# Differential attention in an encoder trunk: the turned map's low part ahead of the combination, the last map's reciprocal between the two stacks, and the copy of K's low part on ScalarE

## The chip, the cores and the metric

The kernel runs as one launch on one core of a Trainium2 chip. The metric is the device time of that launch in microseconds (us), median of several runs. The engines are TensorE (PE, with PEld for its weight loads), VectorE (DVE), ScalarE (ACT), GpSimd (POOL) and SyncE (SP, which starts the DMAs). Each engine works through its own list of instructions in order and waits at semaphores.

## The reference

Two layers over 1024 positions of width 1024, all in float32. Layer 0 mixes tokens by differential attention (8 heads, two softmax maps a head), layer 1 by neighbourhood attention; a gated feed-forward part with a convolution follows each. The change touches only the differential attention:

```
q = q.reshape(B, S, H, 2, dh) * (dh ** -0.5)      # H = 8 heads, 2 maps, dh = 64
s = einsum('bqhcd,bkhcd->bhcqk', q, k)            # two score maps, c = 0, 1
s = s - slopes[h] * |q_pos - k_pos|               # penalty by distance
p = softmax(s, axis=-1)
a = p[:, :, 0] - lam * p[:, :, 1]                 # the combination of the two maps
o = einsum('bhqk,bkhe->bqhe', a, v)               # v has 2*dh = 128 columns
o = rms_norm(o, subln_g) * (1.0 - lambda_init)
```

## The kernel before, in words

TensorE multiplies in a format that rounds its operands, so each operand is held in two parts, a high part (the rounded value) and a low part (the rest), and a product is the sum of two or three matmuls. ScalarE makes the high part by a copy, VectorE the low part by a subtraction.

The attention stage takes one head after another, and a head in 8 steps, step t for the 128 queries of tile t. The order on every engine is written out by hand in a function `head` for each; heads 1 to 6 run it in a loop, head 0 and head 7 have copies of their own. In step t of head h:

- PE: `score(t)` makes the two score maps (4 matmuls of 512 columns for map 0, then 4 for map 1), each after the exponential of its map of the step before is done, since there is one PSUM buffer for each map. Then come 12 or 24 matmuls of the next head's projections (`CHUNKS`), in odd steps the product with V of a pair of tiles (`weigh`), and at the step's end the transposition of the combined map of step t-1 (`turn_map(t-1)`, into the one PSUM buffer `da_tb`). Step 2 also turns V (`turn_v`) between its scores and its projections, through the same buffer. `turn_v` needs the low part of map 0 out of the buffer, and `turn_map(1)` needs V's.
- DVE: `combine` (L616: map 0 divided by its sum plus the scaled map 1, both in SBUF), `take_low` (L608: low part of the transposed map t-2, from PSUM and SBUF), in odd steps `finish_o` (L624), then `bias` twice (L660: adds the penalty and finds the row minimum, maps 0 and 1), in even steps L628, in step 2 the low part of V (L608), last the reciprocal of the row sums (L674), which waits for both exponentials.
- ACT: when due, a projection's result out of PSUM (`take`, L490) and two readings of the product with V (L505, L506), then `take_high` (L495: high part of the transposed map t-2), then the exponentials of both maps (L547). In step 2 V's high part (L495) lies between the two.
- POOL: `scale_map` (L278) multiplies map 1 by its reciprocal and minus lambda, after the reciprocal; `combine` waits for it. In steps 0, 3 and 6 a weight tile for a later head is split right behind it: its high part (L270, here called wh) and its low part (L272, here called wl).

At the end of step 7 the next head's operands are stacked. ACT copies the high parts of K and Q for each map c (L515, L516), POOL doubles K's (L296) and halves the penalty strip (L314), and DVE (`stacks`, L630 to L641) makes for each c K's low part (L635), Q's low part (L638) and a copy of K's low part in the other 64 partitions (L641). Then comes the reciprocal of step 7. `score(0)` of the next head waits for all of that; 10 projection matmuls (`EARLY`) stand ahead of it in heads 0 to 6, none in head 7. In head 7 `combine` already comes after the two biases.

Of the kernel before, what the change touches and what calls it, by code (L numbers as in the profile page):

```python
# [15 lines left out]
F32 = mybir.dt.float32  # L16
F32R = mybir.dt.float32r
ALU = mybir.AluOpType
ACT = mybir.ActivationFunctionType
# [56 lines left out]
def diff_attention_stage(nc, x, w_qkv, lam_vec, subln_g, rpb, Z, OT, XTh, XTl, ident, S, lambda_init, shared_raw, next_tiles):  # L76
# [12 lines left out]
    DH = 64  # L89
    H = D // P  # L90
    QT = S // P
# [14 lines left out]
    with ExitStack() as ctx:  # L106
# [5 lines left out]
        raw = m.sb("raw", [P, 3, S])  # L112
        QS = m.sb("QS", [P, 2, S], F32R)
# [357 lines left out]
        @block.scalar  # L471
        def _(act):
            nc.scalar.preload_act_table(ACT.Exp)
            act.wait_ge(iota_done, 1)

            nc.scalar.activation(strip[:], strip[:], ACT.Abs, scale=0.5).then_inc(strip_ready, 1)

            def x_high_part(t):
                act.wait_ge(x_turned, t + 1)
                nc.scalar.activation(XTh[:, :, t * P:(t + 1) * P], xp[t], ACT.Copy).then_inc(x_high, 1)  # L480

            def w_high_part(j):

                act.wait_ge(w_in[j % 2], 16 * (j // 2 + 1))
                nc.scalar.activation(wh[:, j], wraw[:, j % 2], ACT.Copy).then_inc(w_high, 1)

            def take(h, j):

                act.wait_ge(proj_done, ORDER.index(j) + 1 if isinstance(h, int) and h == 0 else 6 * h + j + 1)
                nc.scalar.activation(raw[:, j // 2, (j % 2) * BANK:(j % 2 + 1) * BANK], bank(h, j)[:], ACT.Copy,  # L490
                                     scale=-(DH ** -0.5) if j < 2 else 1.0).then_inc(proj_out, 1)

            def take_high(i, out):
                act.wait_ge(turned, i + 1)
                nc.scalar.activation(out, tb[:], ACT.Copy).then_inc(t_high, 1)  # L495

            def take_map(h, qt):
                q = qt // 2
                if not (isinstance(h, int) and h == 0 and q < 2):
                    act.wait_ge(pv_done, 4 * h + q - 1)  # L500
                take_high(t_index(h, qt), ATh[:, q % 2, :, (qt % 2) * P:(qt % 2 + 1) * P])

            def ready_o(i):
                act.wait_ge(pv_done, i + 1)
                nc.scalar.activation(sq[:], pb[:, 0:QW], ACT.Square).then_inc(sq_ready, 1)  # L505
                nc.scalar.activation(og[:], pb[:, 0:QW], ACT.Copy, scale=gsub[:, 1:2]).then_inc(og_ready, 1)  # L506

            def stacks(h, after):

                act.wait_ge(proj_out, 6 * h + 4)  # L510
                if after:
                    act.wait_ge(scored[1], 8 * h)
                for c in range(2):
                    a = slice(c * DH, (c + 1) * DH)
                    nc.scalar.activation(KH[a, c], raw[a, 1], ACT.Copy).then_inc(stack_high, 1)  # L515
                    nc.scalar.activation(QS[a, c], raw[a, 0], ACT.Copy).then_inc(stack_high, 1)  # L516

            def head(h, first, last):
                for t in range(QT):
                    n = 8 * h + t  # L520
                    if t in TAKE and t and not last:
                        if TAKE[t] == 0:
                            act.wait_ge(stack_low, 4 * h + 4)
                        if TAKE[t] == 4:
                            act.wait_ge(turned, 9 * h + 2)
                        take(h + 1, TAKE[t])
                    if t == 0 and not first:
                        take(h, TAKE[0])
                    if t % 2 == 0 and (t > 2 or not first):
                        ready_o(4 * h + t // 2 - 2)  # L530
                    if t >= 2:
                        take_map(h, t - 2)
                    elif not first:
                        take_map(h - 1, t + QT - 2)
                    if t == QT - 1 and not last:
                        stacks(h + 1, True)
                    for c in range(2):
                        if t == 2 and c == 1:
                            if not first:
                                act.wait_ge(pv_done, 4 * h)  # L540
                            take_high(9 * h + 1, Vh[:])
                        act.wait_ge(biased[c], n + 1)
                        if t >= 2:
                            act.wait_ge(turned, t_index(h, t - 2) + 1)
                        elif not first:
                            act.wait_ge(turned, t_index(h - 1, t + QT - 2) + 1)
                        nc.scalar.activation(E[:, t % 2, c], Sc[c][:], ACT.Exp, scale=-1.0, bias=mn[:, t % 2, c:c + 1],  # L547
                                             accum_out=den[:, t % 2, c:c + 1]).then_inc(exped[c], 1)

            for t in range(QT // 2):  # L550
                x_high_part(t)
            w_high_part(0)
            w_high_part(1)
            take(0, 0)
            for t in range(QT // 2, 3 * QT // 4):
                x_high_part(t)
            w_high_part(2)
            take(0, 2)
            for t in range(3 * QT // 4, QT):
                x_high_part(t)  # L560
            for j in ORDER[2:4]:
                take(0, j)
            stacks(0, False)
            for j in ORDER[4:]:
                take(0, j)
            act.wait_ge(lam_dots, 2)
            nc.scalar.activation(lams[:, 2:4], lams[:, 0:2], ACT.Exp).then_inc(lam_exps, 1)
            act.wait_ge(g_ready, 1)
            head(0, True, False)
            with act.Fori(1, H - 1) as h:  # L570
                head(h, False, False)
            head(H - 1, False, True)
            ready_o(4 * H - 2)
            take_map(H - 1, QT - 2)
            take_map(H - 1, QT - 1)
            ready_o(4 * H - 1)

        @block.vector
        def _(dve):
# [30 lines left out]
            def take_map(h, qt):  # L610
                at = (slice(None), (qt // 2) % 2, slice(None), slice((qt % 2) * P, (qt % 2 + 1) * P))
                take_low(t_index(h, qt), ATh[at], ATl[at])

            def combine(n, b):
                dve.wait_ge(scaled, n + 1)
                nc.vector.scalar_tensor_tensor(out=E[:, b, 0], in0=E[:, b, 0], scalar=rden[:, b, 0:1], in1=E[:, b, 1],  # L616
                                               op0=ALU.mult, op1=ALU.add).then_inc(combined, 1)
# [9 lines left out]
                dve.wait_ge(sum_done, i + 1)  # L627
                nc.vector.tensor_scalar(ms[:], pb[:, QW:QW + 2], 1.0 / P, RMS_EPS, ALU.mult, ALU.add).then_inc(ms_ready, 1)  # L628

            def stacks(h):  # L630

                for c in range(2):
                    a, b = slice(c * DH, (c + 1) * DH), slice((1 - c) * DH, (2 - c) * DH)
                    dve.wait_ge(stack_high, 4 * h + 2 * c + 1)
                    nc.vector.tensor_tensor(out=KL[a, c], in0=raw[a, 1], in1=KH[a, c].bitcast(F32),  # L635
                                            op=ALU.subtract).then_inc(stack_low, 1)
                    dve.wait_ge(stack_high, 4 * h + 2 * c + 2)
                    nc.vector.tensor_tensor(out=QS[b, c], in0=raw[a, 0], in1=QS[a, c].bitcast(F32),  # L638
                                            op=ALU.subtract).then_inc(stack_low, 1)
                    dve.wait_ge(stack_low, 4 * h + 2 * c + 1)  # L640
                    nc.vector.tensor_copy(KL[b, c], KL[a, c].bitcast(F32)).then_inc(kl_dup, 1)  # L641

            def head(h, first, last):
                for t in range(QT):
                    n = 8 * h + t
                    if (t or not first) and not last:
                        combine(n - 1, (t - 1) % 2)
                    if t >= 2:
                        take_map(h, t - 2)
                    elif not first:  # L650
                        take_map(h - 1, t + QT - 2)
                    if t >= 5 and t % 2 == 1:
                        finish_o(h, (t - 5) // 2)
                    elif t % 2 == 1 and not first:
                        finish_o(h - 1, (t + 3) // 2)
# [12 lines left out]
                    if t == 2:  # L668
                        take_low(9 * h + 1, Vh[:], Vl[:])
                    if t == QT - 1 and not last:  # L670
                        stacks(h + 1)
                    dve.wait_ge(exped[0], n + 1)
                    dve.wait_ge(exped[1], n + 1)
                    nc.vector.reciprocal(rden[:, t % 2], den[:, t % 2]).then_inc(inverted, 1)  # L674

            stacks(0)
            dve.wait_ge(lam_exps, 1)

            nc.vector.scalar_tensor_tensor(out=neglam[:], in0=lams[:, 3:4], scalar=-lambda_init, in1=lams[:, 2:3],
# [1257 lines left out]
```

## Time and profile before

| | us |
|---|---|
| median of 3 runs | 2939.55 |
| their range | 2937.84 to 2942.13 |
| the profiled execution: its time | 2941.45 |
| its span, first to last instruction | 2939.6 |
| PE busy / DVE / ACT / POOL | 2761.2 / 1646.7 / 993.7 / 1244.3 |

The attention stage takes about the first 680 us; its heads 1 to 6 lie between 136 and 593 us and take about 76 us each. PE's busy time counts overlapping, pipelined matmuls, so it says that PE is seldom without work, not that it is at its peak. What matters for the change is where PE waits inside a head, and for which instruction of which engine.

### The profile page before, as it was taken

The page shows a single profiled execution, that of the slowest core. Times are in us where ns is not written, and L with a number is a line of the kernel's source. Part 1 is how long each engine was busy: PE and PEld are TensorE (multiplying, and loading weights), DVE is VectorE, ACT ScalarE, POOL GpSimd, SP SyncE. Part 2 cuts the span into 40 slices and gives each one's busy share as a digit, 9 for nine tenths or more (in the row PEclk, how much of TensorE's full clock was granted, in tenths as well). Part 3 has the DMA queues.
Part 4 walks back from the last instruction along what each step waited for, and adds up shares of the span by engine and source line. Part 5 has one row for each costly group of instructions (what it writes and reads, how often), then busy time and mean ns, then how long its engine had stood idle before and what let it go on. Part 6 is the DMA issues. An engine that isn't in the chain of part 4 may idle for free. (4 is left out here: it accounts for less than half of the span.)

```text
span 2939.6 us, 36441 instructions
## 1 busy us (share of the span) xinstructions
PE 2761.2 (94%) x13387; PEld 2300.0 (78%) x13387; DVE 1646.7 (56%) x2106; ACT 993.7 (34%) x1402; POOL 1244.3 (42%) x890
## 2 busy tenths in 40 slices
PE   7999999967899999999988999998789999999998
PEld 6788888856788888888877888887668888888886
DVE  3666666663564444444473777777475444444447
ACT  3544555442231122222233555555323111222222
POOL 2444444333563333333354566555357233333335
PEclk9999999988999999999999999999899999999999
DMA  3000001225111111111121221211602111111111
GB/s 117 26 27 24 29 29 35 56 67 190 41 47 43 51 54 46 50 48 45 50 79 42 64 51 44 48 44 22 213 13 75 43 43 52 55 43 50 50 43 72
DMA packets 212649, 163.16 MB, mean 56 GB/s; under 512 B 34939, under 2 KB 194251, under 8 KB 212555
## 3 DMA queue, kind: packets, MB, share of 16 engines
q1 hardware_dynamic: 212411, 161.38, 18.6%
q8 instruction: 59, 0.97, 0.1%
q10 hardware_dynamic: 144, 0.52, 0.1%
q14 instruction: 35, 0.29, 0.0%
HBM read 137.24 MB, written 24.64 MB: 55 GB/s over the span
## 5 line engine op out<-in xcount | busy, mean ns | idle before, releaser
L1131 PE MATMUL ff_ph<-XTh,WH 128*128 128x512 f32 x1408 | 549.7, 390 | 6.9 <-PEq L41 6.9
L1131 PE MATMUL ff_ph<-XTl,WH 128*128 128x512 f32 x1408 | 548.9, 390 | 0.0
L1131 PE MATMUL ff_ph<-XTh,WL 128*128 128x512 f32 x1408 | 548.7, 390 | 0.0
L1289 DVE SCALAR_TENSOR_TENSOR ff_C<-ff_H,ff_par,ff_C 128x1024 f32<-128x1024 f32 x88 | 206.5, 2346 | 548.1 <-ACT ff_C L1233 548.1
L1069 POOL TENSOR_SCALAR WH<-raw_weights 128x1024 fp32r<-128x1024 f32 x128 | 142.3, 1111 | 845.6 <-PE ff_ph L1131 488.9
L1071 POOL TENSOR_TENSOR WL<-raw_weights,WH 128x1024 fp32r<-128x1024 f32 x128 | 328.9, 2570 | 10.7
L1131 PEld LDWEIGHTS ff_ph<-XTh,WH 128*128 128x128 f32 x1408 | 265.0, 188 | 62.7 <-issue 7.6
L1131 PEld LDWEIGHTS ff_ph<-XTh,WL 128*128 128x128 f32 x1408 | 265.0, 188 | 55.5
L1131 PEld LDWEIGHTS ff_ph<-XTl,WH 128*128 128x128 f32 x1408 | 265.1, 188 | 54.9
L1229 ACT ACTIVATE ff_H<-ff_ph,ff_par 128x1024 f32<-128x1024 f32 x88 | 98.4, 1118 | 553.6 <-PE ff_ph L1131 553.6
L1282 DVE TENSOR_TENSOR X<-ff_po,X 128x512 f32<-128x512 f32 x288 | 191.6, 684 | 102.5 <-PE ff_po L1145 102.5
L1145 PE MATMUL ff_po<-WH 128*128 128x512 f32 x576 | 228.3, 396 | 4.7 <-DVE X L1282 0.2
L1145 PE MATMUL ff_po<-WH,WL 128*128 128x512 f32 x576 | 224.4, 390 | 0.0
L1145 PE MATMUL ff_po<-WL,WH 128*128 128x512 f32 x576 | 224.4, 390 | 0.0
L547 ACT ACTIVATE da_E<-da_S,da_mn 128x1024 f32<-128x1024 f32 x128 | 142.9, 1117 | 226.4 <-DVE da_mn L660 223.7
L1526 POOL TENSOR_SCALAR na_E<-na_E,na_rden 128x512 f32<-128x512 f32 x128 | 103.8, 811 | 204.8 <-DVE na_rden L1868 204.7
L1612 PE MATMUL na_pa<-XTh,na_wh 128*128 128x512 f32 x360 | 146.1, 406 | 18.8 <-ACT na_raw L1731 11.8
L278 POOL TENSOR_SCALAR da_E<-da_E,da_rden,da_neglam 128x1024 f32<-128x1024 f32 x64 | 76.6, 1197 | 199.6 <-DVE da_rden L674 199.6
L347 PE MATMUL da_pa<-XTh,da_wh 128*128 128x512 f32 x360 | 151.7, 421 | 10.0 <-POOL da_wl L272 3.8
L660 DVE CUSTOM_DVE_ANT_0 da_S<-da_S,da_strip 128x1024 f32<-128x1024 f32 x128 | 153.8, 1241 | 9.2 <-PE da_S L361 8.2
L1243 ACT ACTIVATE WH<-ff_C 128x1024 fp32r<-128x1024 f32 x44 | 46.8, 1063 | 306.5 <-PE ff_po L1145 268.9
L1612 PE MATMUL na_pa<-XTl,na_wh 128*128 128x512 f32 x360 | 143.9, 400 | 0.0
(224 smaller groups left out, 5990.7 us busy)
## 6 DMA issues: line engine op xcount, KB each, us to landing
raw_weights<-in_ffn_w_in SPq DMA_DIRECT2D x88, 512.0 KB, 3.8
raw_weights<-in_ffn_w_out SPq DMA_DIRECT2D x44, 512.0 KB, 3.5
raw_weights<-in_attn_w_qkv SPq DMA_DIRECT2D x24, 512.0 KB
raw_weights<-in_na_w_qkv SPq DMA_DIRECT2D x24, 512.0 KB, 4.2
wo_oraw<-heads_t SPq DMA_DIRECT2D x16, 512.0 KB, 4.6
rpb_rows<-da_rows SPq DMA_DIRECT2D x2, 3840.0 KB, 26.4
na_B<-rpb_rows SPq DMA_DIRECT2D x32, 224.0 KB, 4.2
da_E<-in_x SPq DMA_DIRECT2D x8, 512.0 KB, 6.5
```

The lines of the kernel that those rows point to most:

```text
L347: last = nc.tensor.matmul(out[:], w[:, j // 2, k], x[:, k, t0:t0 + BANK], start=(i == 0), stop=(i == 3 * KT - 1))
L547: nc.scalar.activation(E[:, t % 2, c], Sc[c][:], ACT.Exp, scale=-1.0, bias=mn[:, t % 2, c:c + 1], accum_out=den[:, t % 2, c:c + 1]).then_i ...
L660: nc.vector.tensor_tensor_reduce(out=Sc[c][:], in0=Sc[c][:], in1=strip[:, (QT - 1 - t) * P:(QT - 1 - t) * P + S], scale=1.0, scalar=3.0e38 ...
L1069: nc.gpsimd.tensor_scalar(wh[:, slot], wraw[:, raw_slot], 1.0, 1.0, ALU.mult, ALU.mult).then_inc(w_high, 1)
L1071: nc.gpsimd.tensor_tensor(out=wl[:, slot], in0=wraw[:, raw_slot], in1=wh[:, slot].bitcast(F32), op=ALU.subtract).then_inc(w_low, 1)
L1131: last = nc.tensor.matmul(out[:, at], wt[:, slot, k * P:(k + 1) * P], x[:, k, at], start=(k == 0 and n == 0), stop=(k == KT - 1 and n == 2))
L1145: last = nc.tensor.matmul(po[r % 4][:], a[:, f, t * P:(t + 1) * P], wt[:, slots[f], half * BANK:(half + 1) * BANK], start=(f == 0 and n == ...
L1229: nc.scalar.activation(H[:, parity, 1:S + 1], ph[parity][:].rearrange("p k n -> p (k n)"), ACT.Identity, bias=par[:, 0, bass.ds(idx, 1)])
L1282: nc.vector.tensor_tensor(out=at, in0=po[r % 4][:], in1=at, op=ALU.add).then_inc(added, 1)
L1289: nc.vector.scalar_tensor_tensor(out=c, in0=h[:, 0:S], scalar=tap[1], in1=c, op0=ALU.mult, op1=ALU.add).then_inc(conv_link, 1)
L1526: nc.gpsimd.tensor_scalar(E[:, b], E[:, b], rden[:, b:b + 1], 1.0, ALU.mult, ALU.mult).then_inc(scaled, 1)
L1612: last = nc.tensor.matmul(out[:], w[:, j // 2, k], x[:, k, t0:t0 + BANK], start=(i == 0), stop=(i == 3 * KT - 1))
```

## The change

Three edits in the attention stage. On DVE `take_low` of map t-2 now stands ahead of `combine` of map t-1. The stacks of the last step are cut in two, with the reciprocal between them: stack 0, reciprocal, stack 1. The copy of K's low part (L641) goes from DVE to ACT: for c = 0 behind the two exponentials of step 7, for c = 1 in step 0 of the next head, behind `take_high`. The waits on semaphores keep their meaning.

```diff
+            def double_low(h, c):
+                a, b = slice(c * DH, (c + 1) * DH), slice((1 - c) * DH, (2 - c) * DH)
+                act.wait_ge(stack_low, 4 * h + 2 * c + 1)
+                nc.scalar.activation(KL[b, c], KL[a, c].bitcast(F32), ACT.Copy).then_inc(kl_dup, 1)
...
                         take_map(h - 1, t + QT - 2)
                     if t == QT - 1 and not last:
                         stacks(h + 1, True)
+                    if t == 0 and not first:
+                        double_low(h, 1)
...
+                    if t == QT - 1 and not last:
+                        double_low(h + 1, 0)
...
             stacks(0, False)
+            for c in range(2):
+                double_low(0, c)
...
-            def stacks(h):
-
-                for c in range(2):
...
-                    dve.wait_ge(stack_low, 4 * h + 2 * c + 1)
-                    nc.vector.tensor_copy(KL[b, c], KL[a, c].bitcast(F32)).then_inc(kl_dup, 1)
+            def stacks(h, c):
...
                     n = 8 * h + t
-                    if (t or not first) and not last:
-                        combine(n - 1, (t - 1) % 2)
                     if t >= 2:
                         take_map(h, t - 2)
                     elif not first:
                         take_map(h - 1, t + QT - 2)
+                    if (t or not first) and not last:
+                        combine(n - 1, (t - 1) % 2)
...
                     if t == QT - 1 and not last:
-                        stacks(h + 1)
+                        stacks(h + 1, 0)
                     dve.wait_ge(exped[0], n + 1)
                     dve.wait_ge(exped[1], n + 1)
                     nc.vector.reciprocal(rden[:, t % 2], den[:, t % 2]).then_inc(inverted, 1)
+                    if t == QT - 1 and not last:
+                        stacks(h + 1, 1)
```

On DVE, steps 5 and 6 of a head in the loop. Before (`da_E` is the combination, `da_ATl` the low part, `da_S` the bias):

```order
L674 RECIPROCAL da_rden<-da_den 128x2
L616 SCALAR_TENSOR_TENSOR da_E<-da_E,da_rden 128x1024
L607 REGISTER_ALU
L608 TENSOR_TENSOR da_ATl<-da_tb,da_ATh 128x8x128
L27 REGISTER_ALU
L660 ISA da_S,da_mn<-da_S,da_strip 128x1024
```

and after, where each line number is 7 to 11 higher:

```order
L681 RECIPROCAL da_rden<-da_den 128x2
L618 REGISTER_ALU
L619 TENSOR_TENSOR da_ATl<-da_tb,da_ATh 128x8x128
L627 SCALAR_TENSOR_TENSOR da_E<-da_E,da_rden 128x1024
L27 REGISTER_ALU
L667 ISA da_S,da_mn<-da_S,da_strip 128x1024
```

The low part and the combination have changed places between the reciprocal and the bias, in every step of heads 0 to 6. On DVE at the end of step 7, before:

```order
L635 TENSOR_TENSOR da_KL<-da_raw,da_KH 64x1024
L637 REGISTER_ALU
L638 TENSOR_TENSOR da_QS<-da_raw,da_QS 64x1024
L641 CAST da_KL<-da_KL 64x1024
L634 REGISTER_ALU
L635 TENSOR_TENSOR da_KL<-da_raw,da_KH 64x1024
L637 REGISTER_ALU
L638 TENSOR_TENSOR da_QS<-da_raw,da_QS 64x1024
L641 CAST da_KL<-da_KL 64x1024
L674 RECIPROCAL da_rden<-da_den 128x2
```

and after:

```order
L644 TENSOR_TENSOR da_KL<-da_raw,da_KH 64x1024
L646 REGISTER_ALU
L647 TENSOR_TENSOR da_QS<-da_raw,da_QS 64x1024
L681 RECIPROCAL da_rden<-da_den 128x2
L643 REGISTER_ALU
L644 TENSOR_TENSOR da_KL<-da_raw,da_KH 64x1024
L646 REGISTER_ALU
L647 TENSOR_TENSOR da_QS<-da_raw,da_QS 64x1024
L692 REGISTER_ALU
L692 COMPARE_AND_BRANCH
```

The reciprocal has moved ahead of the second stack and the two copies are gone; the second stack now runs straight into the loop's branch.

## Rows read from the trace of the kernel before

**Rows 1.** Windows of two heads; columns: stretch, length, PE busy, clock, DMA

```profile
364.70:440.60 75.90, 72.20 (x400) 1.00 0.09 28
440.60:517.20 76.60, 73.60 (x401) 0.98 0.16 40
```

**Rows 2.** Waits of PE, 130 to 570 us; columns: total us, times, longest

```profile
PE da_tb L376 <- DVE da_ATl L608: 9.4, 6, 1.6
PE da_S L360 <- ACT da_E L547: 5.0, 6, 0.9
PE da_tb L369 <- DVE da_Vl L608: 3.1, 4, 0.8
PE da_S L360 <- DVE da_KL L641: 2.3, 6, 0.4
```

**Rows 3.** Timeline, PE, heads 4 and 5; columns: start, us, instruction, [idle before]

```profile
390.52 0.48 PE L360 MATMUL da_S<-da_KH,da_QS 128*128 128x512 f32 x1
...
425.42 0.48 PE L360 MATMUL da_S<-da_KH,da_QS 128*128 128x512 f32 x1
...
440.63 0.49 PE L360 MATMUL da_S<-da_KH,da_QS 128*128 128x512 f32 x1 [0.41 <-DVE da_KL L641]
...
447.61 0.50 PE L360 MATMUL da_S<-da_KH,da_QS 128*128 128x512 f32 x1 [0.83 <-ACT da_E L547]
...
448.80 0.50 PE L360 MATMUL da_S<-da_KH,da_QS 128*128 128x512 f32 x1
```

**Rows 4.** Timeline, ACT, head 4: steps 2 and 6 (high parts), step 7

```profile
381.38 1.03 ACT L495 ACTIVATE da_ATh<-da_tb 128x1024 fp32r<-128x1024 f32 x1
...
419.76 1.03 ACT L495 ACTIVATE da_ATh<-da_tb 128x1024 fp32r<-128x1024 f32 x1
...
427.53 1.06 ACT L515 ACTIVATE da_KH<-da_raw 64x1024 fp32r<-64x1024 f32 x1 [0.22 <-PE da_S L361]
```

**Rows 5.** Timeline, DVE, head 4, step 2: bias, V's low part

```profile
384.92 1.22 DVE L660 CUSTOM_DVE_ANT_0 da_S<-da_S,da_strip 128x1024 f32<-128x1024 f32 x1
...
388.39 1.23 DVE L608 TENSOR_TENSOR da_Vl<-da_tb,da_Vh 128x1024 fp32r<-128x1024 f32 x1 [1.00 <-ACT da_Vh L495]
```

**Rows 6.** Timeline, DVE, head 4, steps 5 and 6

```profile
412.04 1.23 DVE L608 TENSOR_TENSOR da_ATl<-da_tb,da_ATh 128x1024 fp32r<-128x1024 f32 x1 [0.82 <-ACT da_ATh L495]
...
413.68 1.22 DVE L660 CUSTOM_DVE_ANT_0 da_S<-da_S,da_strip 128x1024 f32<-128x1024 f32 x1
...
417.49 0.17 DVE L674 RECIPROCAL da_rden<-da_den 128x2 f32<-128x2 f32 x1 [1.35 <-ACT da_E L547]
419.11 2.05 DVE L616 SCALAR_TENSOR_TENSOR da_E<-da_E,da_rden 128x1024 f32<-128x1024 f32 x1 [1.45 <-POOL da_E L278]
421.08 1.21 DVE L608 TENSOR_TENSOR da_ATl<-da_tb,da_ATh 128x1024 fp32r<-128x1024 f32 x1
422.21 1.22 DVE L660 CUSTOM_DVE_ANT_0 da_S<-da_S,da_strip 128x1024 f32<-128x1024 f32 x1
```

**Rows 7.** Timeline, POOL, head 4, step 6: low part of a weight tile

```profile
420.17 3.26 POOL L272 TENSOR_TENSOR da_wl<-raw_weights,da_wh 128x1024 fp32r<-128x1024 f32 x1
```

**Rows 8.** Timeline at 1532 us, DVE and POOL: two instructions that read SBUF twice

```profile
1532.18 3.29 DVE L763 SCALAR_TENSOR_TENSOR X<-X,ff_rstd,ff_gb 128x1024 f32<-128x1024 f32 x1 [0.51 <-POOL ff_rstd L772]
...
1532.05 2.33 POOL L784 TENSOR_TENSOR X<-X,ff_gb 128x1024 f32<-128x1024 f32 x1
```

**Rows 9.** Timeline, DVE, from step 7 of head 4 to step 0 of head 5

```profile
430.30 1.22 DVE L660 CUSTOM_DVE_ANT_0 da_S<-da_S,da_strip 128x1024 f32<-128x1024 f32 x1
...
436.50 0.68 DVE L641 CAST da_KL<-da_KL 64x1024 fp32r<-64x1024 f32 x1
...
438.46 1.22 DVE L638 TENSOR_TENSOR da_QS<-da_raw,da_QS 64x1024 fp32r<-64x1024 f32 x1
...
445.05 1.22 DVE L660 CUSTOM_DVE_ANT_0 da_S<-da_S,da_strip 128x1024 f32<-128x1024 f32 x1
```

**Rows 10.** Timeline, POOL, step 7 of head 4 and step 0 of head 5

```profile
440.71 1.19 POOL L278 TENSOR_SCALAR da_E<-da_E,da_rden,da_neglam 128x1024 f32<-128x1024 f32 x1 [5.20 <-DVE da_rden L674]
```

More of the change, by code:

```diff
@@ L628, in mean_square @@
                 nc.vector.tensor_scalar(ms[:], pb[:, QW:QW + 2], 1.0 / P, RMS_EPS, ALU.mult, ALU.add).then_inc(ms_ready, 1)
-            def stacks(h):
-                for c in range(2):
[L633 to L639, printed above, removed]
-                    dve.wait_ge(stack_low, 4 * h + 2 * c + 1)
-                    nc.vector.tensor_copy(KL[b, c], KL[a, c].bitcast(F32)).then_inc(kl_dup, 1)
+            def stacks(h, c):
+                a, b = slice(c * DH, (c + 1) * DH), slice((1 - c) * DH, (2 - c) * DH)
+                dve.wait_ge(stack_high, 4 * h + 2 * c + 1)
+                nc.vector.tensor_tensor(out=KL[a, c], in0=raw[a, 1], in1=KH[a, c].bitcast(F32),
+                                        op=ALU.subtract).then_inc(stack_low, 1)
+                dve.wait_ge(stack_high, 4 * h + 2 * c + 2)
+                nc.vector.tensor_tensor(out=QS[b, c], in0=raw[a, 0], in1=QS[a, c].bitcast(F32),
+                                        op=ALU.subtract).then_inc(stack_low, 1)
             def head(h, first, last):
@@ L674, in head @@
                     nc.vector.reciprocal(rden[:, t % 2], den[:, t % 2]).then_inc(inverted, 1)
-            stacks(0)
+                    if t == QT - 1 and not last:
+                        stacks(h + 1, 1)
+            for c in range(2):
+                stacks(0, c)
             dve.wait_ge(lam_exps, 1)
```

## The prediction

> **What bounds the kernel now.** I read the windows of single heads first, to see how long a head takes and at which clock: 75.9 us with the clock at full, 76.6 us in a head where the granted clock sank for a while (0.98 on average) [rows 1]. PE is busy for nearly all of it, so what can be won is its waits. The list of PE's waits then says what they are: in each head about 1.6 us for the low part of map 0 (ahead of `turn_v`), 0.8 us for V's low part (ahead of `turn_map(1)`), 0.8 us for an exponential (ahead of `score(1)`), 0.4 us for the copy of K's low part (ahead of `score(0)`) [rows 2]. With the refilling of PE's pipe they cost about 4.5 us a head. The timeline gives the places: the last two are at 440.63 and 447.61 [rows 3]. So PE bounds the long steps, and the loop over DVE, ACT and POOL bounds step 6 to step 2, where the steps are short. In that loop I need four distances. From a bias to the reciprocal: 413.68 to 417.49, 3.81 us. From the reciprocal to the combination: 1.62 us, during which POOL scales. From the reciprocal to the issue of wl in a step with a split: 417.49 to 420.17, 2.68 us [rows 6, 7]. From a bias to the score that waits for its exponential: 445.05 to 447.61, 2.56 us [rows 9, 3].
>
> **Low part ahead of the combination, step 2.** DVE idles 1.45 us while POOL scales [rows 6], and the low part takes 1.13 us to the next start. But the low part needs ACT's high part, and ACT makes that only after the second exponential and after its other readings. In step 2 it ends at 381.38 + 1.03 = 382.41 [rows 4]. The low part of map 0 can then start at 382.45 and `turn_v` follows 1.3 us earlier than now. The bias, however, comes at 382.45 + 1.13 + 1.21 (combination) = 384.79, against 384.92 [rows 5]: 0.1 us earlier. V's high part lies behind the first exponential of that bias, V's low part behind it (388.39), and `turn_map(1)` waits for that. What `turn_v` gains, `turn_map(1)` gives back; step 2 gains 0.1 us. `score(3)` at 390.52 [rows 3] is thus tied to the bias, and a head can be followed from it to the next `score(3)`.
>
> **Steps 3 to 6.** In steps 4 and 5 the high part is late because PE turns the map late; DVE waits for it (0.82 us at 412.04) with the combination already done [rows 6]. Now the combination stands behind the low part, and the bias moves from 413.68 to about 414.8, 1.1 us later. These steps are long and PE does not notice. The reciprocal of step 5 follows at 417.49 + 1.1 = 418.6, and wl is issued 2.68 us behind it, at 421.27. The low part of step 6 is bound by ACT's high part, 419.76 + 1.03 [rows 4], so it starts at 420.83 and the combination is ready at 421.96, 0.7 us after wl began. Before, it was ready at 419.11, beside the short wh, and took 2.05 us instead of 1.28 [rows 6], and wl, queued behind it, took 3.26 us [rows 7]. What a DVE instruction with two inputs in SBUF does when POOL's two-input one has begun is seen at 1532 us: POOL starts 0.13 us ahead, runs its 2.33 us, and the DVE instruction ends 1.09 us after it, 3.29 us in all [rows 8]. So wl holds to 421.27 + 2.33 = 423.60, the combination ends at 424.69, and the bias of step 6 starts at 424.62 instead of 422.21. `score(7)` waits for its exponential: 424.62 + 2.56 = 427.18 instead of 425.42 [rows 3], 1.8 us late, and some 0.3 us more for the second map, whose matmuls start 1.19 us behind the first's as at 448.80 [rows 3]. This wait is new. The same overlap in step 3 costs nothing, since that step is long.
>
> **The stacks.** Everything in step 7 is about 2.1 us late: the bias at 432.4 instead of 430.30. Where the first copy began, 6.20 us after the bias (436.50) [rows 9], there is now the reciprocal, at 438.64, and behind it the low part of K, map 1 (1.22 us). POOL's scaling (1.19 us alone [rows 10], so it is issued 1.62 - 1.2 = 0.4 us after the reciprocal) falls inside this subtraction, starts in earnest at about 439.9 and takes 1.1 us more; the subtraction of Q, which took 1.22 us at 438.46 [rows 9], waits for it in turn and ends at 442.1. `score(0)` could start at 440.63 - 0.57 (its wait and refill) + 2.1 = 442.2: its wait is gone, 0.6 us won. The two copies taken off DVE (0.68 us each) give nothing beyond that. On ACT they cost what its 64x1024 copy costs, 1.06 us [rows 4]; ACT has gaps there, and the second ends at about 441.3. An estimate between 0.68 (the copy on DVE) and 1.22 (the slowest free 64x1024 row) leaves it 0.7 us early at worst, so I take 1.06 and no effect. In step 0 DVE goes on with the low part (442.0) and is ready to combine at 443.15, where the split's wh, held up by Q's subtraction, has ended at 443.0 and wl is issued at 443.09. This is a tie. If wl is first, the combination ends at 443.09 + 2.33 + 1.09 = 446.5, the bias of step 0 comes at 446.4 instead of 445.05 [rows 9], `score(1)` at 449.0 instead of 447.61 [rows 3]: 1.4 us late. If the combination is first, the bias comes at 444.3 and `score(1)` does not wait, 0.4 us late.
>
> The Trainium skill (page "SBUF — State Buffer", section "SBUF: two separate sides") says that the read and write ports shared by VectorE and GpSimd are an exclusive lock: the one that starts first holds them for its whole instruction and the other fully blocks. The trace agrees (3.29 us in rows 8); by that rule 0.06 us decide as well as 1 us, and the tie goes to wl.
>
> **The sum.** Steps 1 and 2 regain 0.2 and 0.1 us, since the scaling now lies beside the low part. A head is then 1.4 - 0.3 = 1.1 us longer, and six times that (from `score(3)` of head 0 to that of head 6) is 6.6 us. Head 0 gains 0.8 us in its step 2, where ACT's high part is early. Head 6 has splits in step 0 alone, and its end leaves `score(0)` of head 7 0.3 us later, because the scaling delays Q's subtraction; head 7 is unchanged. Together +6.1 us. The clock comes on top: before, it sank in two of the six heads, at 0.7 us each [rows 1]. Now each head has two waits of 1.8 to 2.1 us instead of one of 1.6, ahead of stretches that PE bounds, so I estimate three or four dips at about 1.2 us, 2.9 us more than before; the bounds are 0 and 8. So +9.0 us: 2941.45 becomes 2950.4. The profiled execution lies 1.9 us above the median of the runs, so the time is 2948.5 us.
>
> **The rivals.** First: in step 7 POOL doubles K's high part, issued 0.04 us after the combination by my reckoning. If POOL is first, the combination, the bias and both stacks come 0.9 us later, `score(0)` waits 0.9 us, and a head is 2.0 us longer: 12 - 0.5 + 2.9, 2954 us. For it: high part and K's copy follow each other closely on ACT; against it: the order reckoned. Second: the combination of step 0 beats wl. A head is then 0.3 us shorter: -1.8 - 0.5, and about 3 us for the clock, 2940 us. For it: the margin is 0.06 us; against it: DVE must also pass the loop's branch there, which only delays it. Third, on the other side: the combination of step 6 is issued ahead of wl. It would have to be ready 0.7 us earlier, or the reciprocal of step 5 be 0.7 us later than I reckon. Then that step costs 0.6 us instead of 2.1, and with the second rival as well a head is 1.8 us shorter: -10.6 - 0.5, 2928.5 us. Without the second it is 0.4 us shorter, 2937 us. For it: DVE idles 1.45 us in each of those steps; against it: the margin is ten times that of the ties.
>
> **How the numbers follow.** Forecast 0.44 (own range 2943 to 2953), first rival 0.18, second 0.22, third 0.16, half of it the full gain. Slower and faster start at 0.2%, 5.9 us, about what a measurement of this kernel can tell from none. The forecast is slower in 0.36 of its 0.44; with the first rival that makes 0.54. Same: 0.08 of the forecast, 0.18 of the second, 0.05 of the third: 0.31. Faster: the rest, 0.15. The range 2933 to 2955 leaves out the full gain and a dip in every wait.
>
> **What the profile will show.** Right: the combination of steps 3 and 6 takes 2.6 to 3.5 us in heads 0 to 5; PE waits 1.6 to 2 us for an exponential ahead of `score(7)`; the wait of `turn_v` falls below 0.6 us, that of `turn_map(1)` grows to about 2 us; none for K's low part is left in heads 1 to 6. The combination of step 0, 3.4 us or 1.3 us, decides between forecast and second rival. Wrong: a combination of step 6 of about 2 us, or heads shorter than 75.5 us.

## The result, and the profile after

The changed kernel takes 2958.91 us (median of 4 runs, 2958.38 to 2959.47), the kernel before 2940.84 us (4 runs): ratio 1.0058, 95% interval 1.0045 to 1.0071, slower by 17 us. The profiled execution has a span of 2956.6 us against 2939.6.

First the places where PE waits, 130 to 570 us, as in [rows 2]:

```profile
PE da_tb L369 <- DVE da_Vl L619: 11.7, 6, 2.0
PE da_S L360 <- ACT da_E L554: 10.5, 11, 1.3
PE da_S L360 <- DVE da_QS L647: 5.0, 6, 0.9
PE da_tb L376 <- DVE da_ATl L619: 1.4, 6, 0.2
```

The wait of `turn_v` fell from 9.4 to 1.4 us, and that for V's low part grew from 3.1 to 11.7. The waits for exponentials doubled. The PE timeline gives the places, from `score(0)` of head 4 to `turn_map(1)`, and `score(7)` at the end [rows 3]:

```profile
373.78 0.49 PE L360 MATMUL da_S<-da_KH,da_QS 128*128 128x512 f32 x1 [0.82 <-DVE da_QS L647]
380.61 0.50 PE L360 MATMUL da_S<-da_KH,da_QS 128*128 128x512 f32 x1 [0.68 <-ACT da_E L554]
392.41 1.09 PE L376 MATMUL da_tb<-ident,da_raw 128*128 128x128 f32 x8 [0.23 <-DVE da_ATl L619]
398.21 1.09 PE L369 MATMUL da_tb<-ident,da_E 128*128 128x128 f32 x8 [1.96 <-DVE da_Vl L619]
...
435.69 0.50 PE L360 MATMUL da_S<-da_KH,da_QS 128*128 128x512 f32 x1 [1.27 <-ACT da_E L554]
```

Step 6 on DVE and POOL, which answers to [rows 6, 7]:

```profile
429.35 1.22 DVE L619 TENSOR_TENSOR da_ATl<-da_tb,da_ATh 128x1024 fp32r<-128x1024 f32 x1 [2.14 <-ACT da_ATh L495]
430.49 2.70 DVE L627 SCALAR_TENSOR_TENSOR da_E<-da_E,da_rden 128x1024 f32<-128x1024 f32 x1
433.12 1.22 DVE L667 CUSTOM_DVE_ANT_0 da_S<-da_S,da_strip 128x1024 f32<-128x1024 f32 x1
...
429.72 2.39 POOL L272 TENSOR_TENSOR da_wl<-raw_weights,da_wh 128x1024 fp32r<-128x1024 f32 x1
```

POOL's wl begins at 429.72 and ends at 432.11; the combination, issued at 430.49, ends at 433.19, 1.08 us behind it. Next, step 7 (first two rows) and step 0, DVE and POOL; the third and later rows answer to [rows 9, 10]:

```profile
361.43 2.09 DVE L627 SCALAR_TENSOR_TENSOR da_E<-da_E,da_rden 128x1024 f32<-128x1024 f32 x1
...
361.41 1.04 POOL L296 TENSOR_SCALAR da_KH<-da_KH 64x1024 fp32r<-64x1024 f32 x1 [0.89 <-ACT da_KH L515]
...
371.53 2.11 DVE L647 TENSOR_TENSOR da_QS<-da_raw,da_QS 64x1024 fp32r<-64x1024 f32 x1
...
374.82 3.30 DVE L627 SCALAR_TENSOR_TENSOR da_E<-da_E,da_rden 128x1024 f32<-128x1024 f32 x1
...
370.47 2.11 POOL L278 TENSOR_SCALAR da_E<-da_E,da_rden,da_neglam 128x1024 f32<-128x1024 f32 x1 [1.49 <-DVE da_rden L681]
372.55 2.01 POOL L270 TENSOR_SCALAR da_wh<-raw_weights 128x1024 fp32r<-128x1024 f32 x1
374.64 2.39 POOL L272 TENSOR_TENSOR da_wl<-raw_weights,da_wh 128x1024 fp32r<-128x1024 f32 x1
```

POOL led by 0.02 us in step 7 and by 0.18 us in step 0, and each time the combination waited for the whole of POOL's instruction. In between, the scaling, Q's subtraction and wh took turns, each about 0.9 us longer than alone.

The clock is read from windows of heads (length, PE busy, granted clock), and from the rows where it sank, head 5:

```profile
321.10:399.10 78.00, 72.83 (x404) 1.00 0.09 27
399.10:477.60 78.50, 73.28 (x403) 0.99 0.09 27
477.60:556.60 79.00, 73.77 (x403) 0.99 0.28 63
474.00:482.00 8.00, 6.04 (x24) 0.79 0.00 0
```

```profile
476.16 1.75 PE L369 MATMUL da_tb<-ident,da_E 128*128 128x128 f32 x8 [1.96 <-DVE da_Vl L619]
477.56 0.78 PE L360 MATMUL da_S<-da_KH,da_QS 128*128 128x512 f32 x1
```

After the wait of 1.96 us the same eight transpositions took 1.75 us instead of 1.09 and a score matmul 0.78 instead of 0.48: the lower of the two levels, 1.2 GHz. I call such a stretch a dip, and a head without one a clean head. A clean head takes 75.9 us before and 78.0 us after. In six heads (from `score(3)` of head 0 to that of head 6, as all lengths below) that is 12.1 us. The six heads together take 456.3 us before and 471.6 us after, so 3.1 us are the clock's: above six clean heads they were 0.7 us before (two dips) and are 3.8 us now (three dips, 1.3 us each; the first began 1.1 us before these heads). Dips are counted in the one profiled execution, where the larger part of one lies in these six heads. The rest of the span, from the same starts of `score(3)`: head 0 up to its `score(3)` 1.7 us shorter; from there in head 6 to head 7's 2.2 us longer; from there to the first matmul of the output stage 2.2 us longer (windows below, before and then after); all later stages 1.1 us shorter.

```profile
617.80:688.40 70.60, 40.71 (x213) 0.77 0.11 40
```

```profile
633.60:706.40 72.80, 42.65 (x212) 0.73 0.11 38
```

### The profile page after: what moved, and what is told of

Same layout as the page of the kernel before. It is cut to its first block and busy times, and to the rows that moved or that the text cites. A ratio compares the mean times of both kernels' runs of the same rounds, so it can differ in the third digit from the quotient of the medians.

```text
span 2956.6 us, 36453 instructions
## 1 busy us (share of the span) xinstructions
PE 2766.7 (94%) x13387; PEld 2301.0 (78%) x13387; DVE 1659.3 (56%) x2090; ACT 1008.2 (34%) x1418; POOL 1238.1 (42%) x890
## 5 line engine op out<-in xcount | busy, mean ns | idle before, releaser
L278 POOL TENSOR_SCALAR da_E<-da_E,da_rden,da_neglam 128x1024 f32<-128x1024 f32 x64 | 82.7, 1293 | 186.2 <-DVE da_rden L681 186.2
L619 DVE TENSOR_TENSOR da_ATl<-da_tb,da_ATh 128x1024 fp32r<-128x1024 f32 x64 | 78.3, 1224 | 123.8 <-ACT da_ATh L495 123.6
```

## The experiments

The theory: where the combination, or a stack's subtraction, meets a POOL instruction, one shuts the other out; the first edit moves the combination into wl (steps 3 and 6) and into the doubling of K's high part (step 7), the second moves the stack into the scaling. Rivals: the order costs by itself, since the combination now stands behind a late high part; ACT's copies cost; the clock does it.

| kernel | us | ratio (95%) | clean head, us | dips in 6 heads |
|---|---|---|---|---|
| before | | 1 | 75.9 | 2 |
| changed | 2958.9 | 1.0058 (1.0045 to 1.0071) | 78.0 | 3 |
| e1 first edit alone | 2959.3 | 1.0060 (1.0046 to 1.0073) | 77.3 | 5 |
| e2 second alone | 2952.7 | 1.0035 (1.0021 to 1.0049) | 77.5 | 3 |
| e3 third alone | 2935.1 | 0.9978 (0.9969 to 0.9987) | 74.8 | 4 |
| e4 second and third | 2932.5 | 0.9966 (0.9954 to 0.9978) | 74.2 | 3 |
| e5 changed, K's doubling behind the combination | 2955.2 | 1.0050 (1.0036 to 1.0064) | 77.3 | 5 |
| e6 changed, wl of steps 3 and 6 behind it | 2956.2 | 1.0051 (1.0037 to 1.0064) | 77.0 | 5 |
| e7 changed, all behind it | 2935.7 | 0.9984 (0.9975 to 0.9993) | 74.5 | 3 |
| e8 better version | 2918.2 | 0.9924 (0.9910 to 0.9937) | 72.7 | 0 |
| e9 e8 without V first | 2935.9 | 0.9978 (0.9968 to 0.9988) | 73.8 | 5 |
| e10 changed, V first | 2947.7 | 1.0019 (1.0010 to 1.0028) | 76.9 | 0 |

Each was timed against the kernel before on its own chip (medians 2942.3 for e1 to e4, 2940.7 for e5 to e8, 2942.1 for e9 and e10). Where nearly every head has a dip (changed, e1, e5, e6, e7, e9), the clean head is a single one; e4 has two, 74.2 and 74.5.

**e1, the first edit alone.**

```diff
-                    if (t or not first) and not last:
-                        combine(n - 1, (t - 1) % 2)
                     if t >= 2:
                         take_map(h, t - 2)
                     elif not first:
                         take_map(h - 1, t + QT - 2)
+                    if (t or not first) and not last:
+                        combine(n - 1, (t - 1) % 2)
```

> Only the first edit: the low part ahead of the combination; stacks, reciprocal and copy as before. Lock theory (combination and POOL's instructions shut each other out of a shared port): the combination of step 6 falls into wl and takes about 2.7 us, score(7) waits 1.3 us; in step 7 it meets the doubling of K's high part and takes about 2.1 us; in step 0 it meets only wh, as before (2.05 us). A head about 1.4 us longer than before, with the clock +11 to +15 us in all. Rival (the order alone does it, by putting the combination behind a late high part, without any lock): combinations of 1.28 us in steps 6 and 7, score(7) waits 0.3 us, within 3 us of before.

PE's waits in e1, 130 to 570 us:

```profile
PE da_tb L369 <- DVE da_Vl L608: 11.7, 6, 2.0
PE da_S L360 <- DVE da_KL L641: 8.0, 6, 1.4
PE da_S L360 <- ACT da_E L547: 6.4, 5, 1.3
```

The combination takes 2.71 us in step 6, 2.08 in step 7 and 2.05 in step 0, and a clean head is 1.4 us longer, as the theory had it. The whole is 17 us, more than its 11 to 15: five dips followed, and the six heads are 7.8 us longer than six clean ones, where the kernel before loses 0.7. This edit alone loses as much as all three.

**e2, the second edit alone** (the copies stay on DVE inside each stack).

```diff
                     if t == QT - 1 and not last:
-                        stacks(h + 1)
+                        stacks(h + 1, 0)
                     dve.wait_ge(exped[0], n + 1)
                     dve.wait_ge(exped[1], n + 1)
                     nc.vector.reciprocal(rden[:, t % 2], den[:, t % 2]).then_inc(inverted, 1)
+                    if t == QT - 1 and not last:
+                        stacks(h + 1, 1)
```

> Only the second edit: the reciprocal between the two stacks, copies of K's low part still on DVE, combination ahead of the low part. Lock theory: POOL's scaling falls between the subtractions of the second stack and the Q subtraction takes about 2.1 us, the copy behind it is held by wh (about 1.5 us), score(0) starts 1.5 us later than before; the combination of step 0 then falls into wl (about 3.4 us) and score(1) is 1.0 to 1.5 us later: a head 0.8 to 1.5 us longer, +6 to +12 us in all with the clock. Rival (an earlier reciprocal only helps, 3.1 us of DVE work go from ahead of the scaling to beside it): score(1) without its 0.8 us of waiting, -5 to -8 us.

DVE in e2, from the second stack to the combination of step 0:

```profile
367.07 2.11 DVE L641 TENSOR_TENSOR da_QS<-da_raw,da_QS 64x1024 fp32r<-64x1024 f32 x1
369.10 1.52 DVE L644 CAST da_KL<-da_KL 64x1024 fp32r<-64x1024 f32 x1
370.66 3.29 DVE L621 SCALAR_TENSOR_TENSOR da_E<-da_E,da_rden 128x1024 f32<-128x1024 f32 x1
```

All three durations came as expected (2.1, 1.5, 3.4), the wait ahead of `score(0)` rose to 2.3 us, and the loss of 10 us is in the range. The earlier reciprocal brought no gain by itself. Its three dips, behind the waits ahead of `score(0)`, cost nothing that can be seen: heads with one take 77.47 and 77.49 us, heads without 77.45 to 77.50.

**e3, the third edit alone, and e4, the second and third together.** In e3 both stacks stand ahead of the reciprocal; e4 is the changed kernel with the first edit undone (the diff of e1 backwards).

> Only the third edit: the two copies of K's low part on ACT, both stacks ahead of the reciprocal, combination ahead of the low part. Lock theory: nothing new collides, the reciprocal of step 7 comes 1.36 us earlier (two copies of 0.68 us), score(0) loses its wait, score(1) most of its wait, and step 2 follows: a head 1.1 to 1.4 us shorter, -8 to -10 us in all. Rival (ACT's two copies of 1.06 us delay its high part or an exponential and take part in the loss): no gain, -2 to +5 us.

> Second and third edit, without the first (combination ahead of the low part as before). Lock theory: steps 3 to 7 are as before; in step 0 the scaling and the Q subtraction still shut each other out (2.1 us each), the combination meets wh and ends at about the time at which wl begins, so the bias of step 0 comes 1 to 2 us earlier than before: a head 1.0 to 1.9 us shorter, -7 to -12 us in all. If the first edit carries the loss, this one is the faster by 25 to 30 us against the changed kernel. Rival (the loss comes from the second or third edit): at or above the time before.

e3 gained 7 us and e4 10 us, within 1 us of one range and inside the other. PE's waits in e4:

```profile
PE da_tb L376 <- DVE da_ATl L619: 9.4, 6, 1.6
PE da_tb L369 <- DVE da_Vl L619: 2.3, 3, 0.8
PE da_S L360 <- DVE da_QS L647: 1.1, 5, 0.4
```

The waits of step 2 are those of before; those of steps 0 and 1 are nearly gone. ACT's copies cost nothing that can be seen. Undoing the first edit makes the changed kernel 26 us faster: it carries the loss. The second costs 10 us with the copies on DVE, and nothing once they are on ACT: the combination of step 0 then begins at 358.58 in e4, ahead of wl at 359.54, and takes 1.95 us instead of the 3.29 of e2.

**e5 to e7, the changed kernel with POOL held back.** The order on DVE and ACT stays; POOL waits until the combination has ended: in e5 ahead of the doubling of K's high part, in e6 ahead of wl in steps 3 and 6, in e7 ahead of both and of wl in step 0.

```diff
# e5 and e7
-                        double_k(h + 1, (scaled, 8 * h + QT - 1))
+                        double_k(h + 1, (combined, 8 * h + QT - 1))
# e6 and e7, in split, between wh and wl
-            def split(h, j):
+            def split(h, j, after=None):
...
+                if after is not None:
+                    hold(pool, combined, after, pool_passed)
...
-                        split(h + 2, t // 3 - 1)
# e6; e7 has (0, 3, 6), which is the same in these steps
+                        split(h + 2, t // 3 - 1, 8 * h + t if t in (3, 6) else None)
# e7
-                        split(h + 1, 2)
+                        split(h + 1, 2, None if first else 8 * h)
```

> The changed kernel; on POOL the doubling of K's high part waits until the combination of step 6 has ended, instead of the scaling of step 6. Lock theory: the combination in step 7 takes 1.28 us instead of 2.09, everything behind it in the head comes 0.9 us earlier, the wait of 0.8 us ahead of score(0) goes: a head about 0.9 us shorter, -5 to -6 us against the changed kernel (+12 to +13 against the kernel before). Rival (the combination of 2.09 us has slack, since ACT's stacks set the time there): within 1.5 us of the changed kernel.

> The changed kernel; in steps 3 and 6 POOL starts wl only when the combination has ended (step 0 as it is). Lock theory: the combinations of steps 3 and 6 take 1.28 us instead of 2.7, the bias of step 6 comes 1.4 us earlier, PE's wait ahead of score(7) falls from 1.27 to 0.3 us or less: a head 1.0 to 1.5 us shorter, -6 to -9 us against the changed kernel. Rival (the order alone, the late high part, not the port): the wait ahead of score(7) stays above 1 us, within 2 us of the changed kernel.

> The changed kernel with both, and wl of step 0 behind the combination as well: the three places where a combination meets POOL are taken away, the order of DVE and ACT stays. Lock theory: combinations of 1.28 us in all steps; a head 3.3 to 4.2 us shorter than in the changed kernel, -20 to -25 us, so 0 to 7 us below the kernel before. Rival (the order itself costs, by the late high part): stays above the kernel before by 5 us or more.

Combinations, 130 to 600 us (count, busy, mean ns), in the changed kernel, in e6 and in e7:

```profile
L627 DVE SCALAR_TENSOR_TENSOR da_E<-da_E,da_rden 128x1024 f32<-128x1024 f32 x48 | 91.1, 1897 | 0.0
```

```profile
L629 DVE SCALAR_TENSOR_TENSOR da_E<-da_E,da_rden 128x1024 f32<-128x1024 f32 x48 | 78.2, 1629 | 0.0
```

```profile
L629 DVE SCALAR_TENSOR_TENSOR da_E<-da_E,da_rden 128x1024 f32<-128x1024 f32 x49 | 62.5, 1276 | 0.0
```

e7 decides. With every combination at 1.27 to 1.28 us the changed order is 23 us faster than the changed kernel and 5 us faster than before, inside the expected range, though each low part still stands ahead of its combination. So it is not the order by itself, nor ACT, but the meetings with POOL's instructions that the order brings. e5 and e6 shortened a clean head by 0.7 and 0.9 us (0.9 and 1.0 to 1.5 expected), and as totals they missed: 3 to 4 us instead of 5 to 9. Both had five dips, where the changed kernel had three, and their intervals overlap its own. So the evidence is not in their totals but in the rows: in e5 the combination of step 7 takes 1.28 us instead of 2.09 and the wait ahead of `score(0)` falls from 0.8 to 0.3, in e6 the wait ahead of `score(7)` is gone and only those ahead of `score(1)` are left:

```profile
PE da_S L362 <- ACT da_E L556: 4.0, 6, 0.7
```

Step 0 of e7 still has a wait of 0.3 us ahead of `score(0)`, from the scaling beside Q's subtraction, which nothing here took away. A second meeting stayed in every kernel, the one before included: in step 7 Q's subtraction for c = 0 waits for POOL's halving of the strip and takes 2.71 us, against 1.22 for c = 1 in the kernel before. No run took it away, so what it costs is not known. The kernel before, DVE and POOL:

```profile
433.86 2.71 DVE L638 TENSOR_TENSOR da_QS<-da_raw,da_QS 64x1024 fp32r<-64x1024 f32 x1
432.95 2.56 POOL L314 TENSOR_SCALAR da_strip<-da_strip 128x1920 f32<-128x1920 f32 x1 [1.08 <-DVE da_mn L660]
```

**e10, the changed kernel with V's high part first,** for the prediction's step 2: is `turn_map(1)` bound by V's high part behind the first exponential?

```diff
+                    if t == 2:
+                        if not first:
+                            act.wait_ge(pv_done, 4 * h)
+                        take_high(9 * h + 1, Vh[:])
                     for c in range(2):
-                        if t == 2 and c == 1:
-                            ...
```

> The changed kernel with V's high part ahead of both exponentials of step 2, nothing else. If turn_map(1)'s wait of 1.96 us comes from V's high part behind the first exponential: it falls to 0.9 us, a clean head is 76.9 us instead of 77.96, and fewer dips of the clock follow it: -6 to -11 us against the changed kernel, 2948 to 2953 us. Rival (the wait comes from the late bias alone): no change in the wait, 2957 to 2960 us.

Waits in e10, and its window from 130 to 570 us:

```profile
PE da_S L360 <- ACT da_E L554: 10.5, 11, 1.3
PE da_tb L369 <- DVE da_Vl L619: 5.2, 6, 0.9
PE da_S L360 <- DVE da_QS L647: 5.0, 6, 0.9
```

```profile
130.00:570.00 440.00, 416.35 (x2291) 1.00 0.12 32
```

It is. The wait fell from 2.0 to 0.9 us and PE's other waits stayed, yet the time fell by 11 us: a clean head is 1.05 us shorter, six times that are 6.3, and the clock did not sink once in these heads. The waits of 1.3 us ahead of `score(7)` and of 0.9 us ahead of `score(0)` are all still there. So in the changed kernel the dips came from the wait of 2.0 us ahead of `turn_map(1)`, not from the others.

**e8, the better version, and e9, without V first.** e4, with the low part ahead of the combination in steps 1 and 2 only, where POOL has no split; e8 has the edit of e10 as well.

```diff
-                    if (t or not first) and not last:
+                    if (t or not first) and not last and t not in (1, 2):
                         combine(n - 1, (t - 1) % 2)
...
                         take_map(h - 1, t + QT - 2)
+                    if t in (1, 2) and not last:
+                        combine(n - 1, (t - 1) % 2)
```

> A better version: the second and third edit; the low part ahead of the combination only in steps 1 and 2, where no split runs on POOL; and on ACT V's high part ahead of both exponentials of step 2. My reckoning: as the kernel with the second and third edit alone in steps 3 to 0; turn_v 1.3 us earlier, V's high part in the gap ahead of the exponentials, V's low part right behind the two biases, so turn_map(1) 1.1 us earlier: a head 1.1 to 1.3 us shorter than that kernel (2932.5 us), 2923 to 2926 us. Rival (step 2 is bound elsewhere, by the bias alone): 2931 to 2933 us.

> The better version without its third part: second and third edit, the low part ahead of the combination in steps 1 and 2 only, V's high part between the two exponentials as before. If step 2 is bound as predicted (turn_v gains 1.3 us, turn_map(1) gives it back, since V's high part lies behind the first exponential): a clean head 0.2 to 0.5 us shorter than with the second and third edit alone (73.6 to 74.2 us there), turn_map(1) waits about 2 us, 2929 to 2933 us. Rival (the order in steps 1 and 2 is what makes the better version fast): 2918 to 2922 us.

Waits in e8, and its window; then the same window of e9:

```profile
PE da_tb L369 <- DVE da_Vl L619: 5.2, 6, 0.9
PE da_tb L376 <- DVE da_ATl L619: 1.2, 6, 0.2
PE da_S L360 <- DVE da_QS L647: 0.4, 1, 0.4
...
130.00:570.00 440.00, 431.34 (x2422) 1.00 0.14 36
```

```profile
130.00:570.00 440.00, 425.74 (x2349) 0.98 0.12 33
```

e8 takes 2918.2 us: 22 us less than before, 41 us less than the changed kernel, and 5 us less than the low end of what I reckoned. A clean head is 1.5 us shorter than e4's instead of 1.1 to 1.3, and no dip was left; the rest of the 5 us was not followed up. e9 shows that the order in steps 1 and 2 alone wins nothing: its clean head is 0.4 us shorter than e4's, but the wait of 2.0 us is back, with five dips, and it is no faster than e4; at 2935.9 us it lies 3 us above its expected range. So the order of steps 1 and 2 pays only with V's high part first. Whether that edit alone, on e4, would do as much was not run.

## Why the prediction was wrong

The direction was right, and so was the mechanism, combinations shut out by POOL's instructions; but one tie of it went the other way, and the time lies above the range (2955). The steps in turn:

- Step 2: right. The wait of `turn_v` is 0.23 us, that of `turn_map(1)` 1.96; e10 shows the cause.
- Steps 3 to 6: the mechanism right, the size too large. The combination takes 2.72 us at 401.54 and 2.70 us at 430.49 (here 2.73 was reckoned), but the wait ahead of `score(7)` is 1.27 us, where 1.6 to 2 was named as the sign.
- **Step 7: the step that failed.** The forecast let the combination beat POOL's doubling of K's high part by 0.04 us; POOL led by 0.02 us (361.41 against 361.43 above). That was the first rival, with a chance of 0.18, and its price came true: 0.9 us in each head, a clean head 2.0 us longer in place of 1.1, 5.4 us in all. e5 took it away and measured 0.7; its clean head is 1.3 us longer than before, close to the 1.1 of the forecast. This step alone gives 2954 us, still inside the range; the stretch behind head 6 and the correction below took the time out of it.
- Step 0: right. The scaling and Q's subtraction took 2.11 us each and the tie went to wl (3.30 us), as the Trainium skill's rule (page "SBUF — State Buffer", section "SBUF: two separate sides") has it: the one that starts first holds the shared ports for its whole instruction. The trace agrees, with a lead of 0.18 us here and down to one of 0.02 us in step 7.
- The clock in the six heads: right in size, and that was in part luck. I took three or four dips and 2.9 us; there were three and 3.1 us. The reason given was two waits of 1.8 to 2.1 us in each head; there was one of 1.96, and by e10 the other, 1.27 us, had no part. Behind the same waits of 2.0 us e1 and e5 had five dips, which cost 7.8 and 8.0 us.
- **The stretch behind head 6, the second miss.** From its `score(3)` to the output stage 4.4 us were lost where 0.3 were forecast. Half of that, 2.2 us, lies behind `score(3)` of head 7, where the order is the same in all twelve kernels and PE idles for 30 us in each. This stretch takes 70.6 to 71.0 us where the mean clock is 0.76 to 0.79 (before, e3, e4, e5, e7, e9) and 72.1 to 72.8 us where it is 0.73 to 0.74 (changed, e1, e2, e6, e8, e10). The faster ones include e5, which differs from the changed kernel by one wait of POOL, and the slower ones e8, which has none of the new meetings of steps 3, 6 and 7 (windows below, e5 and then e8). PE's busy time makes 1.9 of the 2.2 us (42.65 against 40.71), so they are nearly all the clock's. Which of the two a kernel gets is open, and the forecast had put nothing there. The other half lies ahead of it: the wait ahead of head 7's `score(0)` is 3.36 us (2.34 before, 2.96 in e5, without the tie of step 7). How it divides was not tested.

```profile
633.60:704.50 70.90, 40.97 (x213) 0.76 0.11 40
```

```profile
597.00:669.20 72.20, 42.27 (x213) 0.74 0.11 39
```

From profiled execution to profiled execution, the first rival's price and the rest as forecast give +14.4 us, 2955.9; it was 2958.4. The 2.5 us between are 4.1 us more behind head 6 and 0.4 us more in the six heads, less 0.9 us at the start (1.7 instead of 0.8; open) and 1.1 us in the later stages (open). On top, I took 1.9 us off because the profiled execution before lay so far above its median. That of the changed kernel lies 0.5 us below its own, so the step added an error of 2.4 us. Together: 5.4 for the tie of step 7, 2.5 for the rest of the sum and 2.4 for this step, of the 10.4 us between 2948.5 and 2958.9.

## What to carry to other kernels

Before an instruction with two SBUF inputs on VectorE is moved, write down what GpSimd runs at the time at which it will be ready, not what it runs now: a meeting with a short instruction can become one with a long one. A margin of hundredths of a microsecond in each of six heads is no margin; price both outcomes, and don't call one of them unlikely. When one wait is shortened, look for the instruction behind it in the same step: here the wait of `turn_v` was won in e9 and given back at `turn_map(1)`; with V's high part moved into a gap as well (e8) it was 16 us faster by the ratios.

## What the runs showed of the hardware

- The shut-out goes both ways and passes on in turn: scaling 1.19 to 2.11 us, Q's subtraction 1.22 to 2.11, wh 1.05 to 2.01, one behind the other; each engine's waiting instruction got in before the other's next.
- PE's granted clock sank behind waits of 2.0 us ahead of a group of transpositions (13 of them in the six heads of e1, e5 and the changed kernel), but not once where that wait was 0.9 us and waits of 1.3 us ahead of score matmuls remained (e10). How often it sank behind the same wait differed: three times in six in two kernels (changed, e7), five in four others (e1, e5, e6, e9). Where no wait of 2.0 us stood there, it sank behind others: behind the 1.6 us wait of `turn_v` (before, e3, e4) and the waits of 2.2 to 2.4 us ahead of `score(0)` (e2). What decides that was not tested.
- Time at the lower clock does not cost the same everywhere. In the six heads it was 9.1 us in the changed kernel, which lost 3.8 us by it, and 17.6 us in e1 and e5, which lost 7.8 and 8.0; but 10.2 us in e2, which lost nothing. Why was not tested.
- Head 7 ran its second half in 70.6 to 71.0 us or in 72.1 to 72.8 us with the same PE idle time, at a mean granted clock of 0.76 to 0.79 or of 0.73 to 0.74.
